# Conv gate: place and time of T1, order of VectorE's sums and splits, and place of the residual loads, in a one-core decoder block

## The chip, the core and the metric
One core of a Trainium2 chip runs the whole block in float32. The metric is the device time in microseconds; lower is better. The kernel before took 778.16 us (median of 3 runs, 776.34 to 778.17).

## The reference, cut to what matters
512 tokens, model width 1024, one layer:

```python
proj = rmsnorm(x, attn_norm_g) @ w_in
u_b, u_c, u_x, q, k, v, g_conv, g_attn = split(proj)
y_conv = (u_b * short_conv(u_c * u_x, conv_w)) @ w_conv_out
y_attn = sliding_window_attention(q, k, v, sinks, rel_bias) @ w_attn_out
mixed  = sigmoid(g_conv) * y_conv + sigmoid(g_attn) * y_attn
x = x + mixed @ w_o
x = x + square(relu(rmsnorm(x, mlp_norm_g) @ w_up)) @ w_down      # D_FF = 4096
return rmsnorm(x, final_norm_g)
```

## The kernel before, in words
The first part (to about 232 us of the trace, "the mixer") multiplies by the columns of w_in for q, k, v and the convolution in strips of 256 columns, each strip once its weights (buffers `raw` and `wgt`) are there, and weaves the attention of four blocks of 128 queries (n = 0 to 3, each in four quarters qd) between the strips. The last three strips are S_MIX + 9 to S_MIX + 11 = S_OUT - 1. GpSimd masks the transposed probabilities of each quarter, `mask(n, qd)`.

Then come 13 stages. Each is a product of 512 x 1024 with 1024 x 1024 in seven half-size products (Strassen's way in Winograd's form) instead of eight, named in the order in which they run: M1, N2, M6, M5, M7, M3, N4. The stages are GC (weights of the conv gate), GA (attention gate), CO (w_conv_out), AO (w_attn_out), WO (w_o), and then eight of the MLP, up and down in turn. Each product takes one 512 x 512 operand of weights, in this order: the blocks and sums B11, B21, T2, T1, T3, B22, T4, with T1 = B11 + B12, T3 = B12 + B22, T2 = B11 + T3, T4 = B21 + T2 (T stands for a sum that the kernel makes of blocks of the weights).

- T1 and T3 are summed by the transfer: GpSimd's queue loads one block and, once it has landed, issues a second load that accumulates onto it (lines 662 and 666 for T1; line 643 for T3's second). T2 and T4 are sums on VectorE: `sum_t2` (line 1700), `sum_t4` (line 1717).
- All loads of blocks, of sums of h (`load_sum`, line 531: operands of M7, M6, M5, M3 in GC and GA, made in the mixer and parked in DRAM) and of the residual x (`load_residual`, line 535) are on SyncE's queue, in the order written out there. Each waits until the product that used the place is through (`wait_used`).
- A weight operand is float32 in a place of `home_raw`. ScalarE rounds it into one of two buffers `high` (`high_part`, line 1165), VectorE subtracts to get the rest, `home_lo` (`low_part`, line 1723). The operand of activations is split in the same way: `s_high` (ScalarE, line 1244) and `s_low` (VectorE, line 1778) into five slots `s_hi_tile`, `s_lo_tile`; `s1` to `s4` (lines 1792 to 1813) are VectorE's sums of activations. A product is three passes on TensorE: high x high, low x high, high x low (line 935; the up stages line 896).
- Results: C11, C22, C12 are gathered in `zc11`, `zc22`, `zc12`: ScalarE copies out a product (`copy_out`, line 1268), VectorE adds another (`sum_c11`, `sum_c22` line 1874, `sum_c12` line 1879). N4 waits for `sum_c22` of its own stage, since it is added on top of M7 in the same banks, which `sum_c22` reads. In GA, CO and AO, N2 goes on top of a copy of M1 in another bank: the `seed` (ScalarE, line 1254), two halves, which waits for the gates (`gate_done`) or for the gated corners (`gated`) that still read the bank.
- `gate` (line 1220) is the sigmoid of one of four corners; `gate_conv` (line 1896) multiplies it with a corner of y_conv, `gate_attn` (line 1903) does so for y_attn, `merge` (line 1910) adds. TensorE then transposes the merged corner (line 859) and ScalarE copies it (line 1226), for stage WO. In WO, `drain` (line 1819) adds a product onto the residual `res`, and TensorE transposes it (line 847).

There is no planner: each engine has one list of instructions written out by hand and runs it in order, so an instruction that waits holds up all that is behind it on its engine. Around the change the lists are: ScalarE lines 1271 to 1346, VectorE lines 1926 to 2010, SyncE lines 548 to 583, GpSimd lines 645 to 668. In ScalarE's list, between the sums of GA and the seed of CO, stand: gate (GA, 1), `high` of CO M1, `s_high(CO, M7)`, gate (GA, 2), which waits for `sum_c12(GA)`, `high` of CO N2, gate (GA, 3), seed.

Memory: `home_of` gives each weight operand one of 14 places; place 5 is `one[3]` (in the mixer: `khi` and `vnat`, read until the last strip is through), place 10 is `ring[2]` (in the mixer: half of weight slot 0, read until strip S_MIX + 10 is through). Before, `g_hi` and `g_lo` (the sums of h for M6) and slot 3 of `s_hi_tile` were at `ring[2]`, and T1 of GC, B21 of GA, B12 of CO and T1 of AO at `one[3]`. The residual takes `one[2]` and `one[3]`.

Of the kernel before, what the change touches and what calls it, by code (L numbers as in the profile page):

```python
# [8 lines left out]
F32R = mybir.dt.float32r  # L9
ALU = mybir.AluOpType  # L10
ACT = mybir.ActivationFunctionType

P = 128
# [144 lines left out]
def home_of(s, name):  # L158


    if s == GC:
        return {"B11": 6, "B12": 13, "T3": 13, "T2": 2, "B21": 1, "B22": 1, "T4": 3, "T1": 5}[name]
    if name == "T4":
        return 6 if s < WO else (12, 6)[(s - WO) % 2]
    if s == GA and name == "T1":
        return 13
    turn = {"T3": 0, "B12": 0, "B21": 1, "T1": 2}
    if name in turn:
        return (3, 4, 5)[(s + turn[name]) % 3] if s < WO else (9, 10, 11)[(s - 3 + turn[name]) % 3]
    return {"B11": 0, "B22": 1, "T2": 2}[name] if s < WO else {"B11": 7, "B22": 1, "T2": 8}[name]  # L170
# [39 lines left out]
def build(nc, x, attn_norm_g, w_in, conv_w, w_conv_out, attn_sinks, rel_bias, w_attn_out, w_o,  # L210
          mlp_norm_g, w_up, w_down, final_norm_g, out):
    ctx = ExitStack()
    with ctx:
# [43 lines left out]
        pv_low = place("pv_low", [HD, T])  # L257
        slot_at = [two_at + 2 * KT * T * i for i in range(3)] + [ring_at + 4 * 2048 * 2, two_at + 6 * KT * T]
        s_hi_tile = [place(f"s_hi_tile{i}", [P, 4, 2 * P], F32R, offset=o) for i, o in enumerate(slot_at)]
# [38 lines left out]
        hs_part = place("hs_part", [P, 4, 2 * P], offset=hs_at[0])  # L298
        g_hi, g_lo = (place(n, [P, 4, 2 * P], F32R, offset=ring[2] + o) for n, o in (("g_hi", 0), ("g_lo", BUF // 2)))
        ident = place("ident", [P, P])  # L300
# [185 lines left out]
        def _(sp):  # L486
# [64 lines left out]
            load_block(GC, 1, 0)  # L551
            sp.wait_ge(hs_out, 16 * 8)
            load_sum(HS.index(M6))
            sp.wait_ge(t_ready, 4 * (TB - 1) + 3)
            load_sum(HS.index(M5))
            load_block(GA, 0, 1)
            wait_strip(sp, S_OUT - 1)
            sp.wait_ge(m_lo, 1)
# [14 lines left out]
            load_block(WO, 0, 1)  # L573
            load_residual(0)
            wait_used(sp, AO, M6)
            load_block(WO, 0, 0)
            load_block(WO, 1, 0)
            wait_used(sp, AO, M5)
            load_residual(1)
            wait_used(sp, AO, M3)  # L580
            load_block(WO, 1, 1)
            for s in range(WO + 1, STAGES):
                load_blocks(s)
# [17 lines left out]
        def _(pool):  # L601
# [44 lines left out]
            pool.dma_start(home_rows(home_of(GC, "T3")), weights(GC, 0, 1)).then_inc(t3_base, 16)  # L646
            for n in range(1, TB):
                if n == 2:
                    add_t3(GC)
                for qd in range(QUADS if n < TB - 1 else 2):  # L650
                    mask(n, qd)

            for s in range(STAGES):
                if s > GC:
                    add_t3(s)
                if s == GC:
                    wait_strip(pool, S_OUT - 1)
                elif s == WO:
                    pool.wait_ge(s_lo, part_no(AO, M7) + 1)
                else:  # L660
                    wait_used(pool, s - 1, M7)
                pool.dma_start(home_rows(home_of(s, "T1")), weights(s, 0, 0)).then_inc(t1_base, 16)
                if s == GC:
                    mask(TB - 1, 2)
                pool.wait_ge(t1_base, 16 * (s + 1))
                pool.dma_start(home_rows(home_of(s, "T1")), weights(s, 0, 1), accum_op=ALU.add).then_inc(t1_in, 16)
                if s == GC:
                    mask(TB - 1, 3)

# [371 lines left out]
        def _(act):  # L1041
# [204 lines left out]
            def seed(s):  # L1246

                if s == AO:
                    act.wait_ge(gated, 4)
                else:  # L1250
                    act.wait_ge(gate_done, 4 * s)
                for b in range(2):
                    act.wait_ge(prod, 14 * s + 2 * M1 + b + 1)
                    a(pair[region(s, N2)][:, b, :], pair[region(s, M1)][:, b, :], ACT.Copy
                      ).then_inc((half_copied, copied)[b], 1)

            def copy_out(s, dst, i, scale=1.0):

                act.wait_ge(prod, 14 * s + 2 * i + 2)
                if s == GC:  # L1260
                    act.wait_ge(conv1, 6 * TB)
                    for j in range(2):
                        act.wait_ge(free_dve[j], frees("D", j, S_OUT - 1))
                elif s == AO:
                    act.wait_ge(gated, {M1: 1, M5: 2, M6: 3}[i])
                elif s > WO and i in (M1, M6):
                    act.wait_ge(s_lo, part_no(s - 1, {M1: M6, M6: M5}[i]) + 1)
                a(dst[:, :, :], four(region(s, i))[:, :, :], ACT.Copy, scale=scale).then_inc(copied, 1)
# [112 lines left out]
            def early_squares(b):  # L1381
                act.wait_ge(drained, drained_before(STAGES - 1) + (2 if b < 2 else 5))
                wait(act, ss3_ready, b)
                sum_squares(b, early(b), 0)

            s_high(WO, M6)
            high_part(WO, M6)
            s_high(WO, M5)
# [112 lines left out]
        def _(dve):  # L1501
# [403 lines left out]
            def merge(at_):  # L1905

                dve.wait_ge(weighed, at_ + 1)
                dve.wait_ge(gated, at_ + 1)
                u = four_of(mixed, *CORNERS[at_])
                v.tensor_tensor(u, u, attn_gate(at_), ALU.add).then_inc(mix_done, 1)  # L1910
# [23 lines left out]
            low_part(GC, M7)  # L1934
            sum_t2(GA)
            low_part(GC, M3)
            sum_c22(GC)
            low_part(GC, N4)
            low_part(GA, M1)
            s3(CO)  # L1940
            sum_c12(GC)
# [9 lines left out]
            s_low(CO, M1)  # L1951
            sum_t2(CO)
            low_part(GA, M3)
            s_low(CO, N2)
            s4(CO)
            s_low(CO, M6)
            low_part(GA, N4)
            sum_c22(GA)
            s_low(CO, M5)
            low_part(CO, M1)  # L1960
            s_low(CO, M7)
            sum_c12(GA)
            sum_t4(CO)
            low_part(CO, N2)

            low_part(CO, M6)
            s2(AO)
            s_low(CO, M3)
            gate_conv(0)
            low_part(CO, M5)  # L1970
            s1(AO)
            s_low(CO, N4)
            low_part(CO, M7)
            sum_t2(AO)
            s_low(AO, M1)
            low_part(CO, M3)
            s_low(AO, N2)
            s4(AO)
            sum_c22(CO)
            low_part(CO, N4)  # L1980
            gate_conv(1)
            s_low(AO, M6)
            low_part(AO, M1)
            sum_c12(CO)
            gate_conv(2)
            gate_conv(3)
            sum_t4(AO)
            low_part(AO, N2)

            low_part(AO, M6)  # L1990
            s_low(AO, M5)
            gate_attn(0)
            merge(0)
            low_part(AO, M5)
            s_low(AO, M7)
# [3 lines left out]
            low_part(AO, M3)  # L1999
            sum_t2(WO)  # L2000
            sum_c22(AO)
            gate_attn(1)
            merge(1)
            low_part(AO, N4)
            sum_c12(AO)
# [172 lines left out]
```

## Time and profile before

| | |
|---|---|
| runs | 776.34, 778.16, 778.17 us |
| profiled execution, own time | 777.43 us |
| its span, first to last instruction | 775.7 us |
| TensorE busy (matmul) | 750.6 us, 97% |
| VectorE busy | 648.0 us, 84% |
| ScalarE busy | 418.6 us, 54% |
| GpSimd busy | 81.7 us, 11% |
| mean granted TensorE clock | 0.994 |
| moved by the DMA engines | 131.22 MB, mean 169 GB/s |

"Busy" for TensorE counts pipelined matmuls one over another, so the idle stretches between groups of matmuls are what is to be read. The stages as the trace has them: the mixer up to 232.7 us, GC to 277.7, GA to 321.6, CO to 361.6, AO to 405.8, WO to 454.4, the MLP after that.

### The profile page before, as it was taken

How to read it: one execution, taken by the hardware profiler on the slowest of the kernel's cores; microseconds unless marked ns; L12 is line 12 of the kernel's file. 1: busy time of each engine (PE TensorE's matmuls, PEld its weight loads, DVE VectorE, ACT ScalarE, POOL GpSimd, SP SyncE). 2: the span in 40 equal slices, each digit the busy share in tenths (PEclk: the TensorE clock that was granted, in tenths of full speed). 3: DMA queues.
4: the chain of work that ended last, by engine and by line, in shares of the span. 5: the costliest groups of instructions: out<-in, count | busy, mean ns of one | idle time of the engine just before them, and what ended most of it. 6: DMA issues, size and time to landing. Idle time of an engine off the chain costs nothing.

```text
span 775.7 us, 10469 instructions
## 1 busy us (share of the span) xinstructions
PE 750.6 (97%) x4067; PEld 648.2 (84%) x4067; DVE 648.0 (84%) x749; ACT 418.6 (54%) x533; POOL 81.7 (11%) x117
## 2 busy tenths in 40 slices
PE   8999999999999899899987999999999999999996
PEld 7888888888887788687865799989998899889985
DVE  5766688988897676779969999998699869996997
ACT  7424555444633656554635777554455455545466
POOL 3102000111123001001100100101010101010102
PEclk9999999999999999999999999999999999999999
DMA  7737413161229877576793666777767776777702
GB/s 252 238 95 264 157 55 109 55 163 54 82 108 315 270 181 211 125 199 165 233 255 105 144 181 169 176 203 188 192 170 198 180 207 170 189 192 193 208 6 109
DMA packets 69408, 131.22 MB, mean 169 GB/s; under 512 B 2604, under 2 KB 22132, under 8 KB 69364
## 3 DMA queue, kind: packets, MB, share of 16 engines
q1 hardware_dynamic: 50400, 84.18, 32.5%
q0 software_dynamic: 18752, 46.15, 27.3%
q8 instruction: 30, 0.49, 0.2%
q10 hardware_dynamic: 212, 0.28, 0.1%
q14 instruction: 14, 0.11, 0.0%
HBM read 124.29 MB, written 6.32 MB: 168 GB/s over the span
## 4 chain that ended last, share of the span: by engine, by line
PE 81%; DVE 8%; DMA 7%; issue 2%; ACT 1%; SPq 0%; POOL 0%; DVEq 0%; ACTq 0%
PE pair L935 34%; PE pair L896 21%; PE pair L705 7%; PE pair L707 7%; PE pair L706 7%; DMA home_raw<-in_w_o 3%; DVE home_lo L1723 2%; DMA home_raw<-in_w_attn_out 2%; DMA home_raw<-in_w_in 1%; PE pair L752 1%; DVE s_lo_tile L1778 1%; PE pair L727 1%; DMA xn<-in_x 1%; PE pair L726 1%; PE pair L736 1%
## 5 line engine op out<-in xcount | busy, mean ns | idle before, releaser
L1165 ACT ACTIVATE high<-home_raw 128x2048 fp32r<-128x2048 f32 x91 | 174.2, 1915 | 155.5 <-PE pair L935 101.9
L1723 DVE TENSOR_TENSOR home_lo<-home_raw,high 128x2048 fp32r<-128x2048 f32 x91 | 208.3, 2290 | 45.0 <-ACT high L1165 44.6
L935 PE MATMUL pair<-high,s_hi_tile 128*128 128x512 f32 x440 | 112.4, 396 | 10.0 <-DVE zc L1874 4.7
L935 PE MATMUL pair<-high,s_lo_tile 128*128 128x512 f32 x440 | 110.1, 390 | 0.1
L935 PE MATMUL pair<-home_lo,s_hi_tile 128*128 128x512 f32 x440 | 109.7, 390 | 0.0
L935 PEld LDWEIGHTS pair<-high,s_hi_tile 128*128 128x128 f32 x440 | 82.5, 190 | 29.4 <-DVE zc L1874 5.5
L705 PE MATMUL pair<-h,wgt 128*128 128x512 f32 x256 | 101.5, 397 | 0.0
L707 PE MATMUL pair<-h,wgt 128*128 128x512 f32 x256 | 99.9, 390 | 0.0
L706 PE MATMUL pair<-h,wgt 128*128 128x512 f32 x256 | 99.8, 390 | 0.0
L935 PEld LDWEIGHTS pair<-high,s_lo_tile 128*128 128x128 f32 x440 | 82.4, 188 | 17.6 <-DVE s_lo_tile L1778 0.5
L935 PEld LDWEIGHTS pair<-home_lo,s_hi_tile 128*128 128x128 f32 x440 | 82.3, 188 | 17.6 <-DVE home_lo L1723 0.6
L896 PE MATMUL pair<-h_hi,home_lo 128*128 128x256 f32 x448 | 58.4, 283 | 0.0
L896 PE MATMUL pair<-h_lo,high 128*128 128x256 f32 x448 | 58.4, 283 | 0.0
L896 PE MATMUL pair<-h_hi,high 128*128 128x256 f32 x448 | 58.3, 283 | 0.0
L707 PEld LDWEIGHTS pair<-h,wgt 128*128 128x128 f32 x256 | 48.0, 188 | 10.4
L896 PEld LDWEIGHTS pair<-h_hi,high 128*128 128x128 f32 x448 | 56.0, 192 | 0.3
L706 PEld LDWEIGHTS pair<-h,wgt 128*128 128x128 f32 x256 | 48.2, 188 | 9.2
L896 PEld LDWEIGHTS pair<-h_hi,home_lo 128*128 128x128 f32 x448 | 55.8, 192 | 0.0
L896 PEld LDWEIGHTS pair<-h_lo,high 128*128 128x128 f32 x448 | 55.8, 192 | 0.0
L705 PEld LDWEIGHTS pair<-h,wgt 128*128 128x128 f32 x256 | 48.1, 188 | 9.1
L1509 DVE TENSOR_TENSOR wgt<-raw,wgt 128x1024 fp32r<-128x1024 f32 x33 | 38.9, 1220 | 8.6 <-ACT wgt L1059 8.4
L1059 ACT ACTIVATE wgt<-raw 128x1024 fp32r<-128x1024 f32 x33 | 33.2, 1056 | 21.2 <-PE pair L707 21.1
(212 smaller groups left out, 1004.2 us busy)
## 6 DMA issues: line engine op xcount, KB each, us to landing
raw<-in_w_in SPq DMA_DIRECT2D x34, 512.0 KB, 4.7
home_raw<-in_w_up SPq DMA_DIRECT2D x16, 1024.0 KB, 5.5
home_raw<-in_w_down SPq DMA_DIRECT2D x16, 1024.0 KB, 5.1
home_raw<-in_w_up POOLq DMA_DIRECT2D x12, 1024.0 KB, 8.3
home_raw<-in_w_down POOLq DMA_DIRECT2D x12, 1024.0 KB, 8.5
home_raw<-in_w_in POOLq DMA_DIRECT2D x7, 1024.0 KB, 9.4
home_raw<-in_w_in SPq DMA_DIRECT2D x7, 1024.0 KB, 6.3
home_raw<-in_w_conv_out SPq DMA_DIRECT2D x4, 1024.0 KB, 5.4
```

The source lines that it names most:

```text
L705: mm(bank[j][:, :], wh, rhs[:, 0, k, :], start=(k == 0), stop=False)
L706: mm(bank[j][:, :], wh, rhs[:, 1, k, :], start=False, stop=False)
L707: last = mm(bank[j][:, :], wl, rhs[:, 0, k, :], start=False, stop=(k == KT - 1))
L726: mm(acc, q, khi[:, kg, keys], start=True, stop=False)
L727: last = mm(acc, q, klo[:, kg, keys], start=False, stop=True)
L736: last = nc.tensor.transpose(bank[B_PT][:, c * P:(c + 1) * P], pr[:, qd % 2, i, P:2 * P], ident[:, :])
L896: last = mm(acc[:, f, :], w[:, k, f * P:(f + 1) * P], a_[:, k, :], start=(fresh and kind == 0 and k == 0 and f % 2 == 0), stop=(kind == 2 ...
L935: last = mm(pair[region(s, i)][:, b, :], a_[:, k, b * P:(b + 1) * P], w[:, k, :], start=(fresh and kind == 0 and k == 0), stop=(kind == 2 ...
L1059: a(wgt[weight_slot(s1)][:, 0, 1024 * e:1024 * e + 1024], raw[raw_slot(c1)][:, :], ACT.Copy).then_inc(hi_ready, 1)
L1165: a(high[n % 2][:, :], home_raw[home_of(s, name)][:, :], ACT.Copy).then_inc(m_hi, 1)
L1509: v.tensor_tensor(w[:, 1, 1024 * e:1024 * e + 1024], raw[raw_slot(2 * s1 + e)][:, :], f32(w[:, 0, 1024 * e:1024 * e + 1024]), ALU.subtract ...
L1723: v.tensor_tensor(home_lo[home][:, :], home_raw[home][:, :], f32(high[n % 2][:, :]), ALU.subtract).then_inc(m_lo, 1)
```

## The change
T1 of GC goes to place 10 (`ring[2]`) and is loaded and summed inside the mixer, before the masks (3, 1) to (3, 3), once strip S_MIX + 10 is through. B21 of GA and B12/T3 of CO go with it to place 10; only T1 of AO stays in place 5, and waits for M3 of CO instead of M7. In exchange `g_hi`, `g_lo` and slot 3 go to `one[3]`, so that the load of M6's sums waits for the last strip. On VectorE, `sum_c22` comes before `sum_t2` of the next stage and the low part of N4, and splits, sums and gates change their order. The residual's loads go behind blocks of w_o. Some waits on `gated` are renumbered to the new order of the corners.

```diff
@@ home_of
-        return {"B11": 6, "B12": 13, "T3": 13, "T2": 2, "B21": 1, "B22": 1, "T4": 3, "T1": 5}[name]
+        return {"B11": 6, "B12": 13, "T3": 13, "T2": 2, "B21": 1, "B22": 1, "T4": 3, "T1": 10}[name]
-        return (3, 4, 5)[(s + turn[name]) % 3] if s < WO else (9, 10, 11)[(s - 3 + turn[name]) % 3]
+        return (3, 4, 5 if s == AO else 10)[(s + turn[name]) % 3] if s < WO else (9, 10, 11)[(s - 3 + turn[name]) % 3]
@@ places
-        slot_at = [...] + [ring_at + 4 * 2048 * 2, two_at + 6 * KT * T]
+        slot_at = [...] + [one_at + 6 * KT * T, two_at + 6 * KT * T]
-        g_hi, g_lo = (... offset=ring[2] + o ...)
+        g_hi, g_lo = (... offset=one[3] + o ...)
@@ SyncE
             sp.wait_ge(hs_out, 16 * 8)
+            wait_strip(sp, S_OUT - 1)
             load_sum(HS.index(M6))
             sp.wait_ge(t_ready, 4 * (TB - 1) + 3)
             load_sum(HS.index(M5))
             load_block(GA, 0, 1)
-            wait_strip(sp, S_OUT - 1)
...
             load_block(WO, 0, 1)
-            load_residual(0)
             wait_used(sp, AO, M6)
             load_block(WO, 0, 0)
             load_block(WO, 1, 0)
             wait_used(sp, AO, M5)
-            load_residual(1)
+            load_residual(0)
             wait_used(sp, AO, M3)
             load_block(WO, 1, 1)
+            load_residual(1)
@@ GpSimd
+            for n in range(1, TB - 1):
+                if n == 2:
+                    add_t3(GC)
+                for qd in range(QUADS):
+                    mask(n, qd)
+            mask(TB - 1, 0)
+            wait_strip(pool, S_MIX + 10)
+            t1_first(GC)      # the load of T1's first block
+            t1_second(GC)     # waits for it, then the accumulating load
+            for qd in range(1, QUADS):
+                mask(TB - 1, qd)
+            for s in range(GA, STAGES):
+                add_t3(s)
+                if s == WO:
+                    pool.wait_ge(s_lo, part_no(AO, M7) + 1)
                 else:
-                    wait_used(pool, s - 1, M7)
+                    wait_used(pool, s - 1, M3 if s == AO else M7)
+                t1_first(s)
+                t1_second(s)
@@ ScalarE
-                    act.wait_ge(gated, 4)      # the seed of AO
+                    act.wait_ge(gated, 3)
-                    act.wait_ge(gated, {M1: 1, M5: 2, M6: 3}[i])
+                    act.wait_ge(gated, {M5: 2, M6: 4}[i])
+            high_part(WO, M6)
             s_high(WO, M6)
-            high_part(WO, M6)
@@ VectorE, stage GC
-            sum_t2(GA)
             low_part(GC, M3)
             sum_c22(GC)
             low_part(GC, N4)
+            sum_t2(GA)
+            s3(CO)
             low_part(GA, M1)
-            s3(CO)
             sum_c12(GC)
@@ VectorE, stages GA and CO
             s_low(CO, M1)
-            sum_t2(CO)
             low_part(GA, M3)
             s_low(CO, N2)
             s4(CO)
+            sum_c22(GA)
+            sum_t2(CO)
+            low_part(GA, N4)
             s_low(CO, M6)
-            low_part(GA, N4)
-            sum_c22(GA)
             s_low(CO, M5)
             low_part(CO, M1)
-            s_low(CO, M7)
             sum_c12(GA)
             sum_t4(CO)
             low_part(CO, N2)
+            s_low(CO, M7)
+            s2(AO)
             low_part(CO, M6)
-            s2(AO)
+            gate_conv(0)
+            s1(AO)
+            low_part(CO, M5)
             s_low(CO, M3)
-            gate_conv(0)
-            low_part(CO, M5)
-            s1(AO)
             s_low(CO, N4)
             low_part(CO, M7)
             sum_t2(AO)
+            low_part(CO, M3)
+            sum_c22(CO)
             s_low(AO, M1)
-            low_part(CO, M3)
-            s_low(AO, N2)
-            s4(AO)
-            sum_c22(CO)
             low_part(CO, N4)
             gate_conv(1)
-            s_low(AO, M6)
+            s_low(AO, N2)
             low_part(AO, M1)
             sum_c12(CO)
-            gate_conv(2)
             gate_conv(3)
             sum_t4(AO)
             low_part(AO, N2)
+            gate_conv(2)
+            s_low(AO, M6)
             low_part(AO, M6)
+            s4(AO)
+            gate_attn(0)
             s_low(AO, M5)
-            gate_attn(0)
+            low_part(AO, M5)
             merge(0)
-            low_part(AO, M5)
@@ VectorE, stage AO
             low_part(AO, M3)
-            sum_t2(WO)
             sum_c22(AO)
             gate_attn(1)
             merge(1)
+            sum_t2(WO)
             low_part(AO, N4)
```

## Rows read from the trace of the kernel before

**Rows 1.** The page's head and its part 1: busy, share, instructions
```profile
span 775.7 us, 10469 instructions
...
PE 750.6 (97%) x4067; PEld 648.2 (84%) x4067; DVE 648.0 (84%) x749; ACT 418.6 (54%) x533; POOL 81.7 (11%) x117
```

**Rows 2.** Waits of TensorE, whole span: total us, times, longest
```profile
PE pair L935 <- DVE zc L1874: 8.4, 3, 3.8
```

**Rows 3.** TensorE in order of time: start, us, operation [idle before <-releaser]
```profile
250.50 1.07 PE L752 MATMUL pair<-pt,vs 128*128 128x512 f32 x4
254.13 3.59 PE L935 MATMUL pair<-high,s_hi_tile 128*128 128x512 f32 x8 [2.55 <-ACT high L1165]
...
261.29 2.06 PE L935 MATMUL pair<-high,s_hi_tile 128*128 128x512 f32 x8
...
314.37 5.53 PE L935 MATMUL pair<-high,h 128*128 128x512 f32 x16 [3.75 <-DVE zc L1874]
319.74 1.98 PE L935 MATMUL pair<-home_lo,h 128*128 128x512 f32 x8
321.55 1.98 PE L935 MATMUL pair<-high,s_hi_tile 128*128 128x512 f32 x8
...
356.07 2.11 PE L935 MATMUL pair<-high,s_hi_tile 128*128 128x512 f32 x8 [1.51 <-DVE zc L1874]
...
398.70 2.11 PE L935 MATMUL pair<-high,s_hi_tile 128*128 128x512 f32 x8 [3.16 <-DVE zc L1874]
```

**Rows 4.** Busy time by stretch; the granted clock is "PEclk", or the column behind POOL
```profile
254.10:257.60 3.50, 3.47 (x9) 2.75 (x10) 3.06 (x4) 3.46 (x4) 0.00 (x0) 0.53 1.09 274
314.30:319.80 5.50, 5.43 (x17) 4.31 (x18) 3.71 (x4) 3.81 (x3) 0.00 (x0) 0.69 1.07 212
398.60:402.00 3.40, 2.88 (x15) 2.20 (x16) 3.33 (x4) 0.00 (x0) 0.67 (x1) 1.00 0.97 243
```

**Rows 5.** GpSimd in order of time, 200 to 470 us
```profile
217.21 0.64 POOL L638 TENSOR_SCALAR_AFFINE_SELECT pt<-pt 128x512 fp32r<-128x512 f32 x1 [1.21 <-DVE pt L1657]
...
241.75 1.30 POOL L666 DMA_DIRECT2D home_raw<-in_w_in  x1
```

**Rows 6.** ScalarE in order of time, 215 to 345 us
```profile
252.17 1.91 ACT L1165 ACTIVATE high<-home_raw 128x2048 fp32r<-128x2048 f32 x1 [6.15 <-DMA home_raw<-in_w_in]
...
300.82 1.90 ACT L1165 ACTIVATE high<-home_raw 128x2048 fp32r<-128x2048 f32 x1
...
321.83 1.06 ACT L1220 ACTIVATE gates<-zc 128x1024 f32<-128x1024 f32 x1 [3.68 <-DVE zc L1879]
...
324.60 1.00 ACT L1220 ACTIVATE gates<-pair 128x1024 f32<-128x1024 f32 x1
326.34 0.58 ACT L1254 ACTIVATE pair<-pair 128x512 f32<-128x512 f32 x1 [0.74 <-PE pair L935]
```

**Rows 7.** DMA issues, 250 to 256 us: last number is us to landing
```profile
s_lo_tile<-h_sums SPq DMA_DIRECT2D x1, 512.0 KB, 9.2
```

**Rows 8.** DMA issues, 256 to 262 us
```profile
s_lo_tile<-h_sums SPq DMA_DIRECT2D x1, 512.0 KB, 6.3
```

**Rows 9.** VectorE in order of time, 340 to 460 us
```profile
346.80 2.29 DVE L1700 TENSOR_TENSOR home_raw<-home_raw,home_raw 128x2048 f32<-128x2048 f32 x1 [2.50 <-DMA home_raw<-in_w_attn_out]
...
395.23 2.29 DVE L1700 TENSOR_TENSOR home_raw<-home_raw,home_raw 128x2048 f32<-128x2048 f32 x1 [7.14 <-DMA home_raw<-in_w_o]
397.44 1.22 DVE L1874 TENSOR_TENSOR zc<-zc,pair 128x1024 f32<-128x1024 f32 x1
...
401.09 2.28 DVE L1723 TENSOR_TENSOR home_lo<-home_raw,high 128x2048 fp32r<-128x2048 f32 x1
...
404.51 1.23 DVE L1778 TENSOR_TENSOR s_lo_tile<-mixed,s_hi_tile 128x1024 fp32r<-128x1024 f32 x1
...
428.53 1.22 DVE L1819 TENSOR_TENSOR res<-res,pair 128x1024 f32<-128x1024 f32 x1
```

**Rows 10.** DMA issues, 378.5 to 379.2 us
```profile
home_raw<-in_w_o POOLq DMA_DIRECT2D x1, 1024.0 KB, 16.5
```

More of the change, by code:

```diff
@@ L257, in build @@
         pv_low = place("pv_low", [HD, T])
-        slot_at = [two_at + 2 * KT * T * i for i in range(3)] + [ring_at + 4 * 2048 * 2, two_at + 6 * KT * T]
+        slot_at = [two_at + 2 * KT * T * i for i in range(3)] + [one_at + 6 * KT * T, two_at + 6 * KT * T]
         s_hi_tile = [place(f"s_hi_tile{i}", [P, 4, 2 * P], F32R, offset=o) for i, o in enumerate(slot_at)]
@@ L298, in build @@
         hs_part = place("hs_part", [P, 4, 2 * P], offset=hs_at[0])
-        g_hi, g_lo = (place(n, [P, 4, 2 * P], F32R, offset=ring[2] + o) for n, o in (("g_hi", 0), ("g_lo", BUF // 2)))
+        g_hi, g_lo = (place(n, [P, 4, 2 * P], F32R, offset=one[3] + o) for n, o in (("g_hi", 0), ("g_lo", BUF // 2)))
         ident = place("ident", [P, P])
@@ L646, in _, with t1_first, t1_second @@
             pool.dma_start(home_rows(home_of(GC, "T3")), weights(GC, 0, 1)).then_inc(t3_base, 16)
-            for n in range(1, TB):
+            def t1_first(s):
+                pool.dma_start(home_rows(home_of(s, "T1")), weights(s, 0, 0)).then_inc(t1_base, 16)
+            def t1_second(s):
+                pool.wait_ge(t1_base, 16 * (s + 1))
+                pool.dma_start(home_rows(home_of(s, "T1")), weights(s, 0, 1), accum_op=ALU.add).then_inc(t1_in, 16)
+            for n in range(1, TB - 1):
                 if n == 2:
                     add_t3(GC)
-                for qd in range(QUADS if n < TB - 1 else 2):
+                for qd in range(QUADS):
                     mask(n, qd)
[L653 to L658, printed above, removed]
+            mask(TB - 1, 0)
[7 more added lines that the diff above has]
+                if s == WO:
                     pool.wait_ge(s_lo, part_no(AO, M7) + 1)
                 else:
-                    wait_used(pool, s - 1, M7)
[L662 to L668, printed above, removed]
+                    wait_used(pool, s - 1, M3 if s == AO else M7)
+                t1_first(s)
+                t1_second(s)
             def gain(b):
@@ L1907, in merge @@
                 dve.wait_ge(weighed, at_ + 1)
-                dve.wait_ge(gated, at_ + 1)
+                dve.wait_ge(gated, (1, 2, 4, 4)[at_])
                 u = four_of(mixed, *CORNERS[at_])
```

## The prediction
> **What bounds the kernel now.** First the head of the page: TensorE is busy for 750.6 us of a span of 775.7 [rows 1]. The profiled execution's own time is 777.43 us, so 1.7 us lie around the span, and it is 0.7 us under the median of the runs shown (778.16). A gain is therefore a stop of TensorE that goes, with its wake, and nothing else; ScalarE or VectorE made quicker elsewhere is worth nothing. The second view is what TensorE waited for: three waits on line 1874, `sum_c22`, make up 8.4 us [rows 2]. The third is TensorE's order of time, which gives each stop its place [rows 3]. A product is 24 matmuls of this kind in three groups of eight that start 1.81 us apart (319.74 to 321.55), 5.44 us in all, and a group starts 0.17 us before the one ahead has ended. So a bracket of idle time costs 0.17 us more than it says. The stops that the change touches:
> - A, GC M5: 2.55 idle, and the first eight then last 3.59 instead of 1.98. 2.72 + 1.61 = 4.3 us.
> - B, GA N4: 3.75 idle, and the first 16 take 5.37 us from start to start instead of 3.63. 3.92 + 1.74 = 5.7 us.
> - C, CO N4: 1.51 idle, 1.7 us.
> - D, AO N4: 3.16 idle at 398.70, and after it VectorE, not TensorE, sets the pace until WO M5.
>
> The slow starts in A and B are TensorE's clock: the granted clock of those stretches is 0.53 and 0.69, that is partly the lower level of 1.2 GHz, after a stop; behind the stop of 3.16 us it stayed 1.00 [rows 4].
>
> **A: T1 of the conv gate.** ScalarE waits 6.15 us for that block and starts `high` at 252.17 [rows 6], since the queue of GpSimd issued the accumulating load only at 241.75 [rows 5]. The new place is free once strip S_MIX + 10 is through, and GpSimd ends mask (3, 0) at 217.85 [rows 5], so the first load goes out at about 218. Even with 9.2 us for it [rows 7] and the 16.5 us of the slowest accumulating load [rows 10] T1 is whole at 244; more likely near 236. `high` for M5 then follows the work in front of it (about 246 to 248), and M5 can start at 250.50 + 0.91 = 251.41. On GpSimd mask (3, 1) stands behind the wait for the base load; that ends near 225 to 227, where the mask's data comes anyway. On SyncE, the sums of M6 now stand behind the last strip (231.6 instead of 217.8), and those of M5, GA's B12 and B11 behind them; even with the 9.2 us of [rows 7] they land near 241, before M6 at 244.96 and M5 at 251.41.
> What is late next: the sums of h for M7. Their load waits for the last attention values, at 251.6 before and after. In the trace they needed 9.2 us from the issue at 251.99 [rows 7], until 261.2, and M7 began at 261.29 [rows 3]; the load was hidden by the stop of A, just. M7 will be due at 251.41 + 5.44 = 256.85. In the new order T1's accumulation is out of the crowd, so the load should go like M3's, 6.3 us [rows 8], or a little slower: I take 6.7, M7 at 258.7. A gives 261.29 - 258.7 = 2.6 us. Ends: 0 (again 9.2 us) and 4.4 (no wait at all).
>
> **B: `sum_c22(GA)` before `sum_t2(CO)`, the low part and two parts of CO.** With TensorE unhindered N4 is due at 314.37 - 3.92 = 310.45. `high` for M3 ends at 302.7 [rows 6], and VectorE starts the low part at 302.8 now that the sum of 2.2 us isn't before it. Then low part 2.2, `s_low(CO, N2)` 1.14, `s4` 1.3, `sum_c22` 1.14: ready at 308.6, so the stop goes. But the work put behind it delays `sum_c12(GA)`: `sum_t2` 2.2, low part 2.2, two `s_low` 2.3, low part of CO M1 2.2, `sum_c12` 1.2 (durations as in [rows 9]) end at 318.6. In ScalarE's unchanged list hang on it gate 2, `high` of CO N2, gate 3 and then the seed: 321.83 to 325.60, 3.8 us [rows 6]. The seed starts at 318.7 + 3.8 = 322.5, its first half lands at 323.1, and CO N2, which needs it, is due at 310.45 + 2 x 5.44 = 321.33. In the trace of before this chain had slack (the seed waited for TensorE until 326.34); now it has none: a new stop of 1.8 us at CO N2. B gives 5.7 - 1.8 = 3.9 us. Ends: 5.7, and 2.2 if the new stop also costs clock as A did.
>
> **C: `sum_c22(CO)`.** The same move. `sum_t2(AO)` still stands before it and waits for its load: it started at 346.80 [rows 9], 2.1 us before M3 (356.07 - 1.7 - 5.44 = 348.9), and ends 0.1 us after M3's start; behind it low part and `sum_c22` need 3.4 us, against 5.44 for M3. It is ready about 1.9 us before N4. 1.7 us. The third seed doesn't become late: it now waits for three conv corners only, with the second put behind it.
>
> **D: `sum_c22(AO)`, `gate_attn(1)`, `merge(1)` before `sum_t2(WO)`.** The sum waited 7.1 us for T3 of w_o, which needed 16.5 us from its issue [rows 10], and the three stood behind it, from 397.44 to 401.09, 3.65 us [rows 9]. Now they run in that idle time (N4 is due at 398.70 - 3.33 = 395.37, so M7 ends at 389.93) and N4's transposes don't wait. From `s_low(WO, M1)` at 404.51 to the addition at 428.53, which releases TensorE's transposes before M5, VectorE is never idle for as much as 0.2 us [rows 9], so what counts is how much earlier that `s_low` is. By VectorE it starts 3.65 us earlier; by the other way (N4's first eight matmuls, eight transposes 1.1, a copy 1.03 and `s_high` 1.06 on ScalarE) at 400.6, 3.9 earlier. The later of the two counts: 3.7 if T3 is no earlier, 3.9 at most if the moved residual brings T3 forward. I take 3.8. The other moves cost nothing: residual 0 goes out 10 us later, residual 1 12 us later, needed 25 us after that; the two loads of AO's T1 start 5.4 us later and have 19.9 us (four products less a split of 1.9) until ScalarE must split it for M5, which the 16.5 us of [rows 10] for the second alone would break, but that crowd isn't there; `high(WO, M6)` before its `s_high` fills a wait of ScalarE for the sum.
>
> **Sum.** 2.6 + 3.9 + 1.7 + 3.8 = 12.0 us. 777.4 - 12.0 = 765.4 for a profiled execution, 766.2 against the median. Behind WO M5 TensorE runs without a stop until the last additions, and every load there hangs on its products, so the gain is kept whole.
>
> **Rivals.**
> 1. The two new waits take more: M7's sums land at 261.2 as before (A gives 0), and the stop at CO N2 costs clock (B 2.2): 0 + 2.2 + 1.7 + 3.7 = 7.6, 770.6 us. For it: the 9.2 us are what this trace shows for this very load, and the clock did fall after 2.55 us. Against: the clock held after 1.51 and after 3.16 us, and one big transfer less is in the crowd.
>    The Trainium skill (TensorE: Matmul & The Clock Gate, the section on the HAM clock gate) says that the clock is at its low level by default, that activity releases it and idling gives it back. By that both new gaps may pay 1.7 us, which would make my forecast 769.6. The trace agrees for A and B and not for the stop of 3.16 us.
> 2. Neither new wait comes: 4.3 + 5.7 + 1.7 + 3.9 = 15.6, 762.6 us. For it: the chain of gates needs only to be 1.8 us shorter; against: each step is a row.
> 3. Something that I don't see gives most of it back (VectorE, busy for 84% of the span, is late for another product of CO or AO): B and C come back there, 4 to 6 us, so about 771.
> 4. The other side: the clock, at one of the two new stops (GC M7 or CO N2), stays at 1.2 GHz. At that level a product costs 5.44 us more; to eat the 12.0 us it must stay low for 24 us, over twice the length of a product at that level. The longest wake in the trace cost 1.74 us, a seventh. Three such stretches would be 778 to 782 us.
>
> **Chances.** Forecast 0.56, rival 1 0.2, rival 2 0.1, rival 3 0.11, rival 4 0.03. What a measurement can tell from no change is about 0.3%, 2.3 us. Slower is rival 4, 0.03; same is the 0.03 in which rival 3 gives back ten microseconds instead of five; the rest, 0.94, is faster. The range goes from all of A and B (762) to rivals 1 and 3 with a microsecond for noise: 761.5 to 772.5.
>
> **What would show it.** Of A: GpSimd issues T1's base near 218, TensorE starts GC M5 right behind the values, and waits for M7 until about 258.7; wrong if M7 starts at 256.9 or after 261. Of B: no idle time before GA N4, and 1 to 2 us before CO N2 with the seed's copy on ScalarE as its releaser; wrong if there is none. Of C: none before CO N4. Of D: `zc` of AO before `home_raw` in VectorE's order, M5 of WO 3.8 us nearer to AO M3 than before. The whole is wrong if the stretch up to the last strip, or the eight stages of the MLP, differ in length by more than half a microsecond.

## Result: 765.55 us, and the profile after

The changed kernel took 765.55 us (median of 4 runs, 765.08 to 767.33) against 778.16 us: ratio 0.9845, 95% interval 0.9825 to 0.9866. The profiled execution took 765.08 us with a span of 763.4 us, against 777.43 and 775.7 before. So the span fell by 12.3 us, where 12.0 were forecast, and the median by 12.6.

The changed file has seven lines more, so L942 here is L935 of before, L1261 the seed (L1254), L1707 `sum_t2` (L1700), L1881 `sum_c22` (L1874). First the page's head and part 1 (busy us, share, instructions):

```profile
span 763.4 us, 10469 instructions
...
PE 747.1 (98%) x4067; PEld 647.0 (85%) x4067; DVE 647.8 (85%) x749; ACT 418.6 (55%) x533; POOL 81.6 (11%) x117
```

The work is the same as in [rows 1]; TensorE's busy time fell by 3.5 us all the same, since fewer matmuls ran at the low clock. The waits of TensorE (total us, times, longest), where [rows 2] had 8.4 us on `sum_c22`:

```profile
...
PE pair L942 <- ACT pair L1261: 1.6, 1, 1.6
PE pair L942 <- DMA s_lo_tile<-h_sums: 1.4, 1, 1.4
PE pair L854 <- DVE res L1826: 1.4, 1, 1.4
PE pair L942 <- ACT s_hi_tile L1251: 1.4, 1, 1.4
PE pair L866 <- DVE mixed L1917: 1.2, 1, 1.2
...
```

`sum_c22` has left the list. The first two lines shown are the two new waits of the prediction, on the seed and on the sums of h; the other three are in WO. Now TensorE in order of time at the places of [rows 3]:

```profile
251.46 1.98 PE L942 MATMUL pair<-high,s_hi_tile 128*128 128x512 f32 x8
...
258.45 2.08 PE L942 MATMUL pair<-high,s_hi_tile 128*128 128x512 f32 x8 [1.39 <-DMA s_lo_tile<-h_sums]
...
307.65 3.79 PE L942 MATMUL pair<-high,h 128*128 128x512 f32 x16
...
320.32 1.20 PE L942 MATMUL pair<-high,s_hi_tile 128*128 128x512 f32 x4 [1.63 <-ACT pair L1261]
...
347.65 1.98 PE L942 MATMUL pair<-high,s_hi_tile 128*128 128x512 f32 x8
...
386.78 1.98 PE L942 MATMUL pair<-high,s_hi_tile 128*128 128x512 f32 x8
```

GC M5 starts behind the values (251.46), GA N4, CO N4 and AO N4 (307.65, 347.65, 386.78) have no bracket of idle time and no slow start. Two stops are new: M7 at 258.45, forecast 258.7, and CO N2 at 320.32. GpSimd, against [rows 5]:

```profile
217.84 0.79 POOL L649 DMA_DIRECT2D home_raw<-in_w_in  x1
225.36 1.29 POOL L654 DMA_DIRECT2D home_raw<-in_w_in  x1 [6.73 <-DMA home_raw<-in_w_in]
227.21 1.79 POOL L638 TENSOR_SCALAR_AFFINE_SELECT pt<-pt 128x512 fp32r<-128x512 f32 x1 [0.56 <-ACT pt L1151]
```

Both loads of T1 go out inside the mixer, and mask (3, 1) behind them waits for its data, not for them. ScalarE at the chain of gates, against [rows 6]:

```profile
315.89 1.06 ACT L1227 ACTIVATE gates<-zc 128x1024 f32<-128x1024 f32 x1 [5.12 <-DVE zc L1886]
316.85 1.90 ACT L1172 ACTIVATE high<-home_raw 128x2048 fp32r<-128x2048 f32 x1
318.66 1.00 ACT L1227 ACTIVATE gates<-pair 128x1024 f32<-128x1024 f32 x1
319.69 1.07 ACT L1261 ACTIVATE pair<-pair 128x512 f32<-128x512 f32 x2
```

Gate 2 waits for `sum_c12(GA)`, and the seed starts 3.80 us after it, as the rows of before said, now without waiting for TensorE. VectorE around T3 of w_o, against [rows 9]:

```profile
381.61 1.22 DVE L1881 TENSOR_TENSOR zc<-zc,pair 128x1024 f32<-128x1024 f32 x1 [2.12 <-PE pair L942]
382.87 1.22 DVE L1910 TENSOR_TENSOR gates<-gates,zc 128x1024 f32<-128x1024 f32 x1
384.12 1.22 DVE L1917 TENSOR_TENSOR mixed<-mixed,gates 128x1024 f32<-128x1024 f32 x1
386.64 2.29 DVE L1707 TENSOR_TENSOR home_raw<-home_raw,home_raw 128x2048 f32<-128x2048 f32 x1 [1.29 <-DMA home_raw<-in_w_o]
```

The three stand before the sum, in time in which VectorE waited before.

### The profile page after: what moved, and what is told of

It is laid out like the page before. It is cut to its first block, busy times and chain, and to the rows that moved or that the text cites. A ratio compares the mean times of both kernels' runs of the same rounds, so it can differ in the third digit from the quotient of the medians.

```text
span 763.4 us, 10469 instructions
## 1 busy us (share of the span) xinstructions
PE 747.1 (98%) x4067; PEld 647.0 (85%) x4067; DVE 647.8 (85%) x749; ACT 418.6 (55%) x533; POOL 81.6 (11%) x117
## 4 chain that ended last, share of the span: by engine, by line
PE 86%; DVE 6%; DMA 4%; issue 2%; ACT 1%; SPq 0%; DVEq 0%; ACTq 0%
PE pair L942 35%; PE pair L903 21%; PE pair L712 8%; PE pair L714 8%; PE pair L713 8%; DMA home_raw<-in_w_o 3%; DVE home_lo L1730 2%; PE pair L759 2%; PE pair L734 1%; PE pair L733 1%; PE pair L743 1%; DMA s_lo_tile<-h_sums 1%; DVE s_lo_tile L1785 1%; DMA xn<-in_x 1%; DVE home_raw L1707 1%
## 5 line engine op out<-in xcount | busy, mean ns | idle before, releaser
L942 PE MATMUL pair<-high,s_hi_tile 128*128 128x512 f32 x440 | 110.5, 391 | 4.4 <-ACT pair L1261 1.6
L942 PE MATMUL pair<-home_lo,s_hi_tile 128*128 128x512 f32 x440 | 109.7, 390 | 0.7 <-DVE home_lo L1730 0.7
L942 PE MATMUL pair<-high,s_lo_tile 128*128 128x512 f32 x440 | 110.1, 390 | 0.1
L942 PEld LDWEIGHTS pair<-high,s_hi_tile 128*128 128x128 f32 x440 | 81.7, 188 | 22.3 <-issue 3.6
L942 PEld LDWEIGHTS pair<-home_lo,s_hi_tile 128*128 128x128 f32 x440 | 82.3, 188 | 18.6 <-DVE home_lo L1730 1.5
L942 PEld LDWEIGHTS pair<-high,s_lo_tile 128*128 128x128 f32 x440 | 82.4, 188 | 17.6 <-DVE s_lo_tile L1785 0.5
L714 PEld LDWEIGHTS pair<-h,wgt 128*128 128x128 f32 x256 | 48.1, 188 | 10.4
```

Source lines behind the costliest of these rows:

```text
L714: last = mm(bank[j][:, :], wl, rhs[:, 0, k, :], start=False, stop=(k == KT - 1))
L942: last = mm(pair[region(s, i)][:, b, :], a_[:, k, b * P:(b + 1) * P], w[:, k, :], start=(fresh and kind == 0 and k == 0), stop=(kind == 2 ...
```

## Experiments

The twelve kernels below "changed" are edits of it or of each other (changed_again has no edit); "changed" is the run and the profile above.

| kernel | median us (range) | ratio to before (95%) | span |
|---|---|---|---|
| changed | 765.55 (765.08 to 767.33) | 0.9845 (0.9825 to 0.9866) | 763.4 |
| changed_again | 765.43 (764.08 to 765.85) | 0.9829 (0.9807 to 0.9852) | 764.1 |
| t1_late | 771.27 (770.45 to 772.29) | 0.9921 (0.9896 to 0.9945) | 769.1 |
| c22_ga_late | 769.71 (768.7 to 770.83) | 0.9901 (0.9876 to 0.9927) | 767.3 |
| c22_co_late | 765.54 (765.38 to 766.88) | 0.985 (0.9826 to 0.9874) | 763.7 |
| t2_wo_first | 770.03 (768.09 to 772.25) | 0.9897 (0.9863 to 0.9931) | 769.7 |
| res_early | 765.14 (764.61 to 765.35) | 0.983 (0.9811 to 0.9848) | 763.5 |
| c12_ga_early | 763.11 (762.56 to 763.67) | 0.9806 (0.9787 to 0.9825) | 761.3 |
| t3_behind_sums | 763.28 (762.26 to 764.07) | 0.9803 (0.9784 to 0.9823) | 762.3 |
| both | 761.25 (761.19 to 763.77) | 0.9794 (0.9775 to 0.9814) | 759.5 |
| gate2_early | 761.84 (760.97 to 762.64) | 0.9789 (0.9766 to 0.9811) | 760.1 |
| t4_pool | 765.61 (764.72 to 766.32) | 0.984 (0.9814 to 0.9866) | 763.5 |
| low_n4_first | 761.0 (759.81 to 761.2) | 0.9775 (0.9758 to 0.9791) | 759.3 |

The kernel before was measured beside each group of them, with medians of 777.62 to 778.41 us, so a difference of two medians of less than 1 us says nothing.

**Part A undone: t1_late.**

```diff
             mask(TB - 1, 0)
-            wait_strip(pool, S_MIX + 10)
+            mask(TB - 1, 1)
+            wait_strip(pool, S_OUT - 1)
             t1_first(GC)
+            mask(TB - 1, 2)
             t1_second(GC)
-            for qd in range(1, QUADS):
-                mask(TB - 1, qd)
+            mask(TB - 1, 3)
```

> The changed kernel, with T1 of the conv gate loaded as late as before (first load after the last strip, masks (3,0) and (3,1) ahead of it), in its new place; all else as changed. Theory (the gains of A, B, C and D are separate and add up): TensorE stops before GC M5 again, M5 starts near 254.1 with a slow first group, M7 at 261.3 instead of 258.5, and the 2.8 us stay lost to the end: span 766.2 instead of 763.4, some 2.8 us slower than the changed kernel. The wait for M7's sums is hidden again. Rival (slack behind: a late stage is absorbed by the stop at CO N2 or by VectorE's chain in WO): the end moves by less than 1 us.

It lost 5.7 us, not 2.8: nothing is absorbed behind, as the theory says, but the stop is larger than before the change, so A is not a part that adds to the others by itself. TensorE in its order of time:

```profile
256.25 3.78 PE L943 MATMUL pair<-high,s_hi_tile 128*128 128x512 f32 x8 [5.65 <-ACT high L1173]
259.83 3.18 PE L943 MATMUL pair<-high,s_lo_tile 128*128 128x512 f32 x8
262.85 1.98 PE L943 MATMUL pair<-home_lo,s_hi_tile 128*128 128x512 f32 x8
```

M5 starts at 256.25, 2.1 us later than before the change, and 16 matmuls take 6.60 us instead of 3.63. Against changed that is 4.8 us at M5 and 3.0 of clock, less 1.6 for M7's wait (hidden again), 6.2 in all; at CO N2 the trace is 6.1 us behind. The mixer of this execution was 1.0 us shorter, though (the last values start at 249.54, against 250.50 before and 250.55 in changed). From the last values to M7 it took 15.1 us, against 10.8 before the change and 7.9 in changed. So the early T1 is not a part that can be left out: without it this stretch is 4.3 us longer than in the old kernel, 3.1 of them wait and 1.3 clock.

T1's accumulating load went out at 241.07 and took 13.2 us to landing where it took 10.4 before. M6's sums (1 MB), which the change put at this place, had landed by then (at 236.86), but two blocks of GA that were issued behind them landed at 244.45 and 248.27, against 242.99 and 245.64 before, and so ran beside the accumulating load for longer. That this is why it was slower is read from these landings and not shown: a late T1 with M6's sums in their old place was not run.

**Part B undone: c22_ga_late.**

```diff
             s_low(CO, M1)
+            sum_t2(CO)
             low_part(GA, M3)
             s_low(CO, N2)
             s4(CO)
-            sum_c22(GA)
-            sum_t2(CO)
-            low_part(GA, N4)
             s_low(CO, M6)
+            low_part(GA, N4)
+            sum_c22(GA)
             s_low(CO, M5)
             low_part(CO, M1)
+            s_low(CO, M7)
             sum_c12(GA)
```

> The changed kernel, with VectorE's order between GA and CO as before (sum_t2(CO) first, sum_c22(GA) behind the low part of N4 and a split, s_low(CO, M7) ahead of sum_c12). Theory: the stop before GA N4 is back (3.9 us with 1.7 us of clock behind it) and the new one of 1.8 us before CO N2 is gone: 3.8 us slower than the changed kernel, span 767.2. Rival (the stop at CO N2 isn't caused by this order): both stops are there, 5.7 us slower, span 769.1.

```profile
258.84 2.08 PE L942 MATMUL pair<-high,s_hi_tile 128*128 128x512 f32 x8 [2.12 <-DMA s_lo_tile<-h_sums]
311.52 5.53 PE L942 MATMUL pair<-high,h 128*128 128x512 f32 x16 [3.33 <-DVE zc L1881]
```

These are its only stops between 240 and 345 us: the one before GA N4 is back with its slow start, the one before CO N2 gone. The span is 3.9 us longer, of which 0.4 lie in M7's wait. The theory holds, the rival (both stops) falls.

**Part C: c22_co_late.**

```diff
             sum_t2(AO)
+            s_low(AO, M1)
             low_part(CO, M3)
+            s_low(AO, N2)
             sum_c22(CO)
-            s_low(AO, M1)
             low_part(CO, N4)
             gate_conv(1)
-            s_low(AO, N2)
```

> The changed kernel, with sum_c22(CO) behind the two splits s_low(AO, M1) and s_low(AO, N2) and the low part of M3; s4(AO) stays late. Theory: sum_c22(CO) is ready 2 x 1.14 us later than now, that is about at the time at which N4 is due or up to 0.6 us behind it, since now it is ready at 345.4 and N4 starts at 347.65: 0 to 0.6 us slower than the changed kernel; the rest of the 1.7 us of part C came from s4(AO) (1.2 us) having left that place. Rival (C was the order of sum_c22 and the low part alone): the full 1.7 us are lost.

No stop before CO N4, and 765.54 us: no change. `sum_c22(CO)` ended 2.1 us later against N4 than in changed, at 347.84, and N4 started at 348.01: it had over 2 us of room, as the theory says, and the two splits need not have left its front. Against before, this kernel differs in that stretch by `s4(AO)` gone from it (1.15 us from start to start), and in its trace T3 of AO landed 8.16 us after its issue instead of 8.72, so `sum_t2(AO)` started 2.62 us before M3 instead of 2.07. The two make up the 1.7 us of the stop; neither was run by itself.

**Part D undone: t2_wo_first.**

```diff
             low_part(AO, M3)
+            sum_t2(WO)
             sum_c22(AO)
             gate_attn(1)
             merge(1)
-            sum_t2(WO)
             low_part(AO, N4)
```

> The changed kernel, with sum_t2(WO) ahead of sum_c22(AO), gate_attn(1) and merge(1) again. Theory: VectorE waits for T3 of w_o until 386.6 before it can do the three, N4 of AO starts 3.3 us later and s_low(WO, M1) 3.65 us later: 3.7 us slower than the changed kernel, span 767.1. Rival (the moved residual load is what helped, since T3 would land late without it): little or nothing is lost by the order alone, under 1.5 us.

```profile
259.28 3.65 PE L942 MATMUL pair<-high,s_hi_tile 128*128 128x512 f32 x8 [2.03 <-DMA s_lo_tile<-h_sums]
322.71 1.20 PE L942 MATMUL pair<-high,s_hi_tile 128*128 128x512 f32 x4 [1.63 <-ACT pair L1261]
...
391.71 3.14 PE L942 MATMUL pair<-high,s_hi_tile 128*128 128x512 f32 x8 [2.38 <-DVE zc L1881]
```

The span is 6.3 us longer, but 2.4 of them are there at CO N2 (322.71 against 320.32), ahead of the edit: the wait for M7's sums was 0.6 us longer in this execution and cost clock, 1.7 us. Behind it the edit cost 3.9 us. That is the number of the theory, but the trace reaches it by two causes:

```profile
398.49 1.23 DVE L1785 TENSOR_TENSOR s_lo_tile<-mixed,s_hi_tile 128x1024 fp32r<-128x1024 f32 x1 [0.99 <-ACT s_hi_tile L1251]
```

VectorE's chain alone would have brought `s_low(WO, M1)` 2.9 us later than in changed (T3 of w_o landed after 15.8 us instead of 16.6). The other 1.0 us is this wait for ScalarE: the granted clock fell behind the stop before N4, and N4's first matmuls and the transposes, on which ScalarE's copy and `s_high` hang, took 4.35 us from start to start instead of 2.61. Of its four runs two have a mean granted clock of 0.998 and took 768.09 and 768.65 us, 2.5 and 3.1 us over changed; the others have 0.994 and 0.995 and took 771.40 and 772.25 us. The median, 4.5 us over changed, lies between the two kinds. The rival (under 1.5 us) falls.

**The residual's place: res_early.**

```diff
             load_block(WO, 0, 1)
+            load_residual(0)
             wait_used(sp, AO, M6)
...
             wait_used(sp, AO, M5)
-            load_residual(0)
+            load_residual(1)
             wait_used(sp, AO, M3)
             load_block(WO, 1, 1)
-            load_residual(1)
```

> The changed kernel, with the two residual loads where they were before (residual 0 behind w_o's B12, residual 1 after AO M5). T3 of w_o needed 16.5 us from its issue before and about 16.7 us in the changed kernel, so the move did not bring it forward. Theory: no effect, T3 lands within 1 us of now, the end within 0.4 us of the changed kernel. Rival (the move pays, since the crowd around T3 would be larger without it now that T1 and T3 are issued closer to it): T3 lands 1.5 us or more later, AO N4's last group and all behind it are late, 1 to 2 us slower.

T3 of w_o landed 15.6 us after its issue, against 16.6 in changed; 765.14 against 765.55 us. The move is worth nothing.

**The new stop at CO N2 taken away: c12_ga_early.**

```diff
             low_part(GA, N4)
+            sum_c12(GA)
             s_low(CO, M6)
             s_low(CO, M5)
             low_part(CO, M1)
-            sum_c12(GA)
```

> The changed kernel, with sum_c12(GA) directly behind the low part of GA N4 and so ahead of s_low(CO, M6), s_low(CO, M5) and the low part of CO M1. Theory (the stop before CO N2 comes from the chain sum_c12(GA), gate 2, high of CO N2, gate 3, seed): sum_c12 ends at 311.3 instead of 315.8, the seed waits for TensorE again, the stop of 1.63 us goes: 1.8 us faster than the changed kernel, span 761.6; the low part of CO M1 ends at 315.8, 0.9 us before it is needed. Rival (the two splits or the low part become late in their turn): a new stop of about 1 us before CO M1's last group or at CO M6, gain under 1 us.

ScalarE in its trace, same chain as above:

```profile
311.55 1.06 ACT L1227 ACTIVATE gates<-zc 128x1024 f32<-128x1024 f32 x1 [0.63 <-DVE zc L1886]
313.49 1.92 ACT L1172 ACTIVATE high<-home_raw 128x2048 fp32r<-128x2048 f32 x1 [0.88 <-PE pair L942]
315.31 1.01 ACT L1227 ACTIVATE gates<-pair 128x1024 f32<-128x1024 f32 x1
318.02 0.58 ACT L1261 ACTIVATE pair<-pair 128x512 f32<-128x512 f32 x1 [1.71 <-PE pair L942]
```

The seed has 1.7 us of room again, TensorE has no stop there, the span is 2.0 us shorter and the time 2.4. The chain of the prediction's part B is shown.

**The wait for M7's sums: t3_behind_sums.**

```diff
             for s in range(GA, STAGES):
+                if s == GA:
+                    pool.wait_ge(hs_in[HS.index(M7)], 32)
                 add_t3(s)
```

> The changed kernel, in which GpSimd issues the accumulating load of GA's T3 (now 247.4 us) only once the sums of h for GC M7 have landed. Theory (the stop before GC M7 comes from sharing the DMA engines with that accumulating load): the sums, issued at 251.65, land 1.3 us or more earlier, near 256.9, and M7 starts at 256.9 to 257.2 instead of 258.45; T3 is issued near 257 and lands near 266, before sum_t2(GA) at 268.4. 1.3 to 1.6 us faster than the changed kernel. Rival (the 6.3 us from issue to landing are latency and issue, not sharing): M7 still starts later than 258.0, gain under 0.4 us.

The second load of M7's sums now landed 4.5 us after its issue instead of 6.3, and M7 started at 257.02 without a stop: sharing with the accumulating load was the cause. It repeats: 6.3 to 7.0 us in the seven executions in which T3's load went out ahead of the sums (changed's 6.3 is the least), 4.3 to 4.9 us in the five in which it went out behind them. T3, issued at 256.94, took 12.6 us where it had taken 8.6 from 247.44, so `sum_t2(GA)` waited 2.7 us and GA N2 0.19. Span 1.0 us shorter, time 2.3; the profiled execution is the slowest of the four.

**Both: both.**

```diff
+            (the edits of c12_ga_early and of t3_behind_sums)
```

> Both edits, sum_c12(GA) early and GA's T3 behind M7's sums. Theory: the gains add, 3.1 us faster than the changed kernel, span 760.3, no stop before GC M7 above 0.4 us and none before CO N2. Rival (time gained at M7 is taken back at CO N2 or by VectorE's chain in WO, which does not depend on the sums): only 1.8 us.

Span 3.9 us shorter, 761.25 us: the gains add, neither of the two stops is left. It is more than the 3.1 expected, since the mixer was 0.3 us shorter and T3 of w_o landed after 15.4 us instead of 16.6, which gave 0.3 us in WO.

**VectorE's chain in WO: gate2_early and t4_pool.**

```diff
             sum_c12(AO)
-            s_low(WO, M1)
             gate_attn(2)
             merge(2)
+            s_low(WO, M1)
             low_part(WO, M1)
```

> The kernel of the run before with both edits (sum_c12(GA) early, GA's T3 behind M7's sums), and in stage AO gate_attn(2) and merge(2) ahead of s_low(WO, M1). Theory (in WO VectorE's chain sets the pace up to M5): s_low(WO, M1) waits 0.66 us for ScalarE there, and the two fill that wait: WO M5 0.7 us earlier, span 758.8, 0.7 us faster than both edits alone. Rival (TensorE's transposes and the split of N2 set the pace, not VectorE): no change.

```diff
             merge(3)
-            sum_t4(WO)
+            dve.wait_ge(t_sum, 2 * WO + 2)
             low_part(WO, N2)
@@ GpSimd, between t1_first(WO) and t1_second(WO)
+            wait_used(pool, AO, M7)
+            pool.wait_ge(b21_in, 16 * (WO + 1))
+            pool.wait_ge(t_sum, 2 * WO + 1)
+            g.tensor_tensor(t4, b21, t2, ALU.add).then_inc(t_sum, 1)
```

> As gate2_early, with sum_t4(WO) taken from VectorE and given to GpSimd, ahead of the accumulating load of T1 of w_o. Theory (VectorE's chain sets the pace and the two engines work side by side): the sum leaves 2.2 us of the chain; on GpSimd it takes about 10.6 us (four times the 2.65 us of its 128x512 product) from 384.3 to 395, before VectorE asks for it at 395.6; WO M5 2.2 us earlier, span 756.6. Rival (they hinder each other: beside a mask of 1.70 instead of 0.64 us on GpSimd a VectorE split took 2.72 instead of 2.28): VectorE loses 2 to 4 us in that stretch and T4 comes late, 0 to 4 us slower than gate2_early. T1 is whole 10 us later in either case, needed 5 us after that.

gate2_early gained nothing (761.84 against 761.25). In its trace VectorE waits for T3 of w_o until 383.28, 1.27 us later than in both, and M5's transposes come 0.64 us later: the landing of T3 sets the start of the chain, and it scatters. From `sum_t2(WO)` to M5's transposes the trace has 31.05 us against 31.68, 0.63 us less, near the 0.7 expected; the time doesn't show it. t4_pool was 3.8 us slower than gate2_early. GpSimd and VectorE in its trace:

```profile
385.09 6.51 POOL L682 TENSOR_TENSOR home_raw<-home_raw,home_raw 128x2048 f32<-128x2048 f32 x1 [15.06 <-DVE home_raw L1715]
```
```profile
384.83 2.28 DVE L1738 TENSOR_TENSOR home_lo<-home_raw,high 128x2048 fp32r<-128x2048 f32 x1
387.03 1.22 DVE L1894 TENSOR_TENSOR zc<-zc,pair 128x1024 f32<-128x1024 f32 x1
388.28 4.40 DVE L1918 TENSOR_TENSOR gates<-gates,zc 128x1024 f32<-128x1024 f32 x1
```

GpSimd's sum took 6.5 us, less than the 10.6 expected, and T4 came in time. But one product of 1.22 us on VectorE took 4.40: it ended 1.1 us after GpSimd's sum, as if it had started then. From `sum_t2(WO)` to the low part of WO N2 VectorE took 17.0 us against 16.0 in gate2_early: 3.2 lost at this product, less the 2.2 of the sum that was gone from its list. The larger loss came by way of TensorE:

```profile
395.13 2.08 PE L950 MATMUL pair<-high,s_lo_tile 128*128 128x512 f32 x4 [3.21 <-DVE s_lo_tile L1793]
```
```profile
404.83 1.23 DVE L1793 TENSOR_TENSOR s_lo_tile<-mixed,s_hi_tile 128x1024 fp32r<-128x1024 f32 x1 [2.96 <-ACT s_hi_tile L1259]
```

TensorE stopped for 3.21 us (0.86 in gate2_early) for the split behind the product, and then ran at a granted clock of 0.50 from 395.1 to 401.0. So the last transposes of AO started at 401.61 instead of 397.21, of which the longer stop is 2.5 us, and VectorE waited 2.96 us for the split on ScalarE behind them.

**The rest of that wait: low_n4_first.**

```diff
             merge(1)
-            sum_t2(WO)
             low_part(AO, N4)
+            sum_t2(WO)
@@ SyncE: the residual loads as in res_early
```

> As gate2_early, with the low part of AO N4 ahead of sum_t2(WO) and the two residual loads back in their places of before. In gate2_early VectorE waited 1.75 us for T3 of w_o (0.19 in the kernel with both edits), so its landing, which scatters by over 1 us, sets the pace from there. Theory: the low part (2.2 us) fills that wait whatever T3 does, and the low part of WO M1 starts 1.1 us earlier than with both edits alone; WO M5 1.1 us earlier, span 758.4 to 758.9, about 1 us faster than both edits. Rival (T3 lands 1 us later with the residual in front, or TensorE's transposes set the pace): no change against both edits, span 759.5 to 760.

`sum_t2(WO)` started at 384.61 without waiting. From `sum_c22(AO)` (378.75, against 378.08 in both) to M5's transposes (413.45, against 413.69) it is 0.9 us shorter, near the 1.1 expected. But GA's T3 took 13.9 us in this execution, so that `sum_t2(GA)`, `sum_c12(GC)` and with them the seed of GA came late and TensorE waited 1.3 us. With a mixer 0.6 us shorter the span gained 0.2 us only. At 761.0 us (0.9775) it is the fastest kernel, and both can't be told from it.

**The spread: changed_again.** No edit.

> The changed kernel itself once more, beside the two others and on the same chip, for its spread: 765.5 us within 0.5, span 763.4; the wait before GC M7 between 1.4 and 2.1 us, since in the five profiles so far with the same transfers up to there it was 1.39, 1.46, 1.84, 2.03 and 2.1.

765.43 us, and a wait of 1.64 us for M7's sums; the span, 764.1, was 0.7 us longer than in changed. Against it the interval of low_n4_first lies wholly lower.

## Why the prediction was right

| step | forecast | measured |
|---|---|---|
| A: M7 starts | 258.7 | 258.45 |
| A: gain | 2.6 | 2.8 |
| B: stop before GA N4 | gone | gone |
| B: new stop before CO N2, on the seed | 1.8 | 1.63 idle, 1.8 from start to start |
| B: gain | 3.9 | 3.8 |
| C: gain | 1.7 | 1.9 |
| D: gain | 3.8 | 3.8 |
| sum | 12.0 | 12.3 |

The gains are differences of starts. CO N2: 326.99 in the trace of before, 320.32 after, 6.67 less the 2.84 of M7. AO M1: 361.64 to 353.10, 8.54. The products of WO from M5 on, and the end: 12.3.

- Bound. A stop of TensorE that goes is kept to the end: from WO M5 to the last instruction the traces of before and after are both 345.0 us long.
- A. Right: the second load of the sums took 6.3 us, where 6.7 was taken, and T3's load beside it is the reason that it wasn't less (t3_behind_sums); with T1 late again it took 10.8 us (t1_late), so T1's place is what took it from before's 9.2. That M7 came 0.2 us ahead of the forecast is luck: the wait before M7 was 1.39 us in changed and 1.46 to 2.13 us in six other executions with the same transfers. The forecast put the move of M6's sums at nothing. That holds for the change as a whole only: with T1 late the same stretch is 4.3 us longer than in the old kernel (t1_late).
- B. Right, both in what goes and in what comes; each step of the chain of gates was at its time within 0.2 us, and c12_ga_early shows it as the cause.
- C. Right in size and in what it did, but the move takes 3.4 us of VectorE's work from in front of `sum_c22` where 1.7 was needed; c22_co_late shows that the two splits need not have left.
- D. Right (undone, VectorE's chain costs 2.9 us and the clock 1.0 in t2_wo_first), and of its two ends the nearer one to no help from the residual: T3 took 16.6 us as before, and the move of the residual, held open as a small gain, gave none (res_early).
- Rival 1 (770.6 us) asked for 9.2 us at M7's sums and for clock at the new stops. Neither came in the profile of changed, but the second came in t2_wo_first: a stop of 2.03 us at M7 cost 1.7 us of clock. One of changed's own four runs may have had the same: 767.33 us at a mean granted clock of 0.995, the other three 0.998 or 0.999; of that run there is no trace. Rival 2 is what the two edits of both made true, 761.25 us where it said 762.6.
- The direction and size of rival 4 (clock low for long) were seen nowhere; the longest wake was 3.0 us, behind a stop of 5.65 us.

## What to carry to other kernels

When a stop is taken out of the critical engine, list what the engines beside it do in the same time: the next wait (here a seed behind a sum that had been pushed back, and a load that the stop had hidden) can be computed from the rows of before. Once known, each was taken out here by moving one instruction or one load. An accumulating load of 1 MB took 8 to 17 us here from issue to landing, and what was issued in that time could land later, so moves of loads must be judged together. In an in-order list put work whose data are there ahead of a sum that waits for a transfer with scattering landing times. And when a number comes out as expected, look whether its causes do: the 3.9 us of t2_wo_first were 2.9 of the chain and 1.0 of clock.

## What was unexpected of the hardware

- The clock after a stop. Idle times behind which the granted clock fell: 2.55 and 3.75 us before; 2.03 and 2.38 (t2_wo_first), 3.21 (t4_pool), 3.33 (c22_ga_late), 5.65 (t1_late). It held after 3.16 us before, and after 1.39 to 2.13 in the others. The granted clock of the stretch behind 2.03 us (busy us of each engine, then the clock):

```profile
259.20:262.90 3.70, 3.62 (x9) 2.88 (x10) 2.29 (x1) 1.18 (x2) 0.00 (x0) 0.54 1.04 402
```

  0.54 is almost wholly the lower of its two levels, 1.2 GHz, and 0.6 us of idle time more than in changed made a difference of 2.4 us at CO N2. The length of a stop alone doesn't decide it: at this very place the clock held after 2.12 (c22_ga_late) and 2.13 us (c22_co_late). By the Trainium skill (TensorE: Matmul & The Clock Gate, on the HAM clock gate) idling gives the clock back and activity releases it. The seven falls agree with that; why 3.16 us was survived and 2.03 us was not, no run here shows.
- GpSimd against VectorE. The 4.40 us above are the only disturbed one of three VectorE instructions beside GpSimd's sum; the first had begun before it, the second reads one operand from PSUM. By the Trainium skill (SBUF — State Buffer, the section on the two separate sides) a VectorE instruction with two SBUF inputs and a GpSimd instruction that reads SBUF take the same ports as a lock, and the later one blocks until the other has ended. The trace agrees: GpSimd's sum ended at 391.60, the product with two SBUF inputs at 392.68. The sum itself was issued beside the low part of AO N4 (two SBUF inputs, until 387.11); if it could start only then, its own time was 4.5 of its 6.5 us, an estimate from these rows.
- The same accumulating load of 1 MB took 8.6 us from 247.44 in changed, and 11.3 to 13.9 us when issued at 255.8 to 257.0, in five kernels, by what else was in flight.
